# Adaptive modulation in a 256-token, ten-stage transformer kernel: from sums over partitions on TensorE to one fused multiply-and-add per 128 outputs on VectorE

## The chip, the cores and the metric

The kernel runs on one core of a Trainium2 chip, as one launch. The metric is the device time of that launch in microseconds. Each core has engines with queues of their own: TensorE (PE in the profile, its weight loads PEld), VectorE (DVE), ScalarE (ACT), GpSimd (POOL) and SyncE (SP, which only issues DMAs here). The engines wait for each other through counting semaphores.

## The reference

A sequence of 256 tokens with 1024 features passes through two layers of a first block (feed-forward, mixer, feed-forward) and two layers of a second block (mixer, feed-forward). The change is about the second block's modulation, which depends only on a vector `c` of 1024 numbers and not on the tokens:

```python
c_act = jax.nn.silu(c)
for l in range(DEPTH):                       # DEPTH = 2
    mod = (c_act @ w_ada[l] + b_ada[l])[:, None, :]      # w_ada[l]: 1024 x 6144
    shift_a, scale_a, gate_a, shift_f, scale_f, gate_f = jnp.split(mod, 6, axis=-1)
    h = rmsnorm(x, g_mix_pre[l]) * (1.0 + scale_a) + shift_a
    y = hybrid_mixer(h, ...)
    x = x + gate_a * rmsnorm(y, g_mix_post[l])
    h = rmsnorm(x, g_ffn_pre[l]) * (1.0 + scale_f) + shift_f
    x = x + gate_f * rmsnorm(swiglu_2(h, w_gate_up[l], w_down[l]), g_ffn_post[l])
```

The modulation's weight is 2 x 1024 x 6144 numbers of 4 bytes, 50 MB. Everything is float32.

## The kernel before

**Stages.** `STAGES` (line 21) lists ten: `f0 a0 f1 f2 a1 f3 b0 f4 b1 f5`. An `f` stage is a feed-forward (F = 2816, in 11 groups of 256), an `a` stage a mixer of the first block, a `b` stage one of the second. Tokens are two tiles of 128.

**Matmuls in three parts.** A float32 weight piece of 128 x 1024 (512 KB) is loaded by SP into one of six buffers `raw`. ScalarE copies it, rounded, to a high part (`Wh` or `QTh`, line 1253), VectorE subtracts to get the low part (`Wl` or `QTl`, line 1645), and TensorE multiplies three times (`three`, lines 820 to 822). SP may load the next piece into a buffer when VectorE has made its low part (`w_lo`). This splitting stream is most of the work of ScalarE and VectorE.

**Order.** It is written out by hand: `walk(s, engine)` gives the list of events of a stage for each engine. In an `f` stage the events are `gu` (gate and up product of a group and a token tile: 24 matmuls of 128x512 into PSUM bank 4 or 5), `turn` (two transposes by TensorE, line 886) and `down` (12 matmuls). There are 22 `gu` in a stage; `gu_in` numbers them 0 to 21. After a `gu` ScalarE takes the Silu (line 1332, function `gate`), VectorE multiplies by the up half (line 1738, `product`), TensorE turns the result, ScalarE (1356) and VectorE (1756) split it in two parts, and TensorE does `down`. The results of `turn` go to PSUM banks 6 and 7 in turn; `ring_no` numbers their uses, and the semaphore `f_z` says that a bank was read.

**Modulation.** It is spread over the four feed-forward stages k = 0 to 3 (`f0 f1 f2 f3`), half a layer in each. ScalarE's queue issues 24 loads of 512 KB in each of them (line 1318) into two buffers in `BT`. Such a load holds two blocks of 128 input rows by 512 outputs. VectorE multiplies a block by the Silu of c, one number for each partition, and adds it to `acc` (128 x 512; line 1727 for the first of eight blocks, line 1730 for the seven others). `ada_to(n)` says how many blocks are done by the n-th `gu`: 8 blocks for every 3 of them. After eight blocks `acc` still has to be summed over its 128 partitions: ScalarE makes a high part (1347), VectorE a low part (2070), TensorE multiplies both by a matrix of ones (`ada_sums`, lines 849 and 850, on one of the two `turn` banks), VectorE adds the bias (1749), and ScalarE's queue stores 512 numbers to a scratch row in HBM (1341). That makes 6 such groups in a stage, 24 in all. Before each `b` stage SP reads four rows of the scratch back as columns of 128 partitions x 8 (line 782), and VectorE's `columns` makes the scales out of them; the two gates are read back as rows (lines 796).

**Around it.** Before the weights of an `a` stage go on, SP waits for the modulation's last store (line 772 with the load at 775), as the buffers in `BT` are needed. At the start ScalarE loads `c` as 128 x 8 (line 1567) and takes its Silu (1569) before the first `turn_x`; the activation table is loaded there.

## Time and profile before

| | |
|---|---|
| Time, three runs | 1705.37, 1710.27, 1711.13 us; median 1710.27 us |
| Profiled execution, first to last instruction (span) | 1699.3 us |
| Own time of the profiled execution | not listed; the span is 11.0 us under the median of the three runs |
| Mean granted TensorE clock | 0.993 of full speed |
| Instructions | 22248 |
| HBM read | 327.32 MB, mean 193 GB/s |

A busy share is a mean over ten stages of different kinds. A matmul's row says when it started and how long it was in the engine; the next one starts before it ends, so the distance between two starts (here 0.22 to 0.23 us for 128x512) says what one more matmul costs, not its duration.

### The profile page before, as it was taken

The numbers are of one execution on the slowest core, as the hardware profiler recorded it, in microseconds if no ns is written. First come the engines' busy times: TensorE is split into PE (matmuls) and PEld (weight loads), VectorE is DVE, ScalarE is ACT, GpSimd is POOL, SyncE is SP. The second block draws the span as 40 slices with busy tenths as digits, with TensorE's granted clock in tenths as the row PEclk, the third lists the DMA queues.
The fourth block names the chain that finished last, engine by engine and source line by source line (L and its number), as shares of the span: only waits on it lengthen the run. The fifth ranks groups of instructions, "written<-read, shape, count | busy, mean of one in ns | idle before, by whom it ended". The sixth has DMA issues, their size and how long they took to land.

```text
span 1699.3 us, 22248 instructions
## 1 busy us (share of the span) xinstructions
PE 1633.9 (96%) x8104; PEld 1352.9 (80%) x8104; DVE 1194.3 (70%) x1833; ACT 930.5 (55%) x1789; POOL 90.6 (5%) x155
## 2 busy tenths in 40 slices
PE   8999998899999999999899999989999989999998
PEld 6888877688888888877688887778888878878887
DVE  6777688777776777779787776776655576675553
ACT  6445567654445444567664445766544367674342
POOL 0000111100000000021010000000000000010000
PEclk9999999999999999999999999989999999999999
DMA  8787633277866887734168784522665552246551
GB/s 321 266 294 260 222 104 124 87 266 256 275 233 207 276 275 257 244 111 144 51 231 273 260 273 144 180 100 87 211 198 175 169 180 94 100 155 222 198 181 62
DMA packets 100107, 329.87 MB, mean 194 GB/s; under 512 B 18800, under 2 KB 19312, under 8 KB 99488
## 3 DMA queue, kind: packets, MB, share of 16 engines
q1 hardware_dynamic: 85504, 276.59, 48.3%
q10 hardware_dynamic: 14496, 51.87, 9.2%
q8 instruction: 66, 1.08, 0.2%
q14 instruction: 41, 0.34, 0.1%
HBM read 327.32 MB, written 1.10 MB: 193 GB/s over the span
## 4 chain that ended last, share of the span: by engine, by line
PE 46%; DVE 6%; ACT 2%; POOL 1%; issue 1%; DVEq 0%; POOLq 0%; ACTq 0%
PE PS L820 14%; PE PS L822 14%; PE PS L821 13%; PE PS L974 1%; DVE Wl L1645 1%; PE PS L886 1%; DVE QTl L1645 1%; POOL st L2142 1%; PE PS L994 1%; DVE PTl L1841 1%; DVE st L1810 1%; PE PS L969 0%; PE PS L837 0%; ACT WK L1369 0%; ACT WK L1380 0%
## 5 line engine op out<-in xcount | busy, mean ns | idle before, releaser
L1645 DVE TENSOR_TENSOR Wl<-raw,Wh 128x1024 fp32r<-128x1024 f32 (+1 forms) x316 | 370.6, 1204 | 44.8 <-ACT Wh L1253 43.9
L820 PE MATMUL PS<-Wh,Hh 128*128 128x512 f32 (+2 forms) x936 | 368.4, 394 | 10.0 <-DVE Hl L1708 3.5
L822 PE MATMUL PS<-Wh,Hl 128*128 128x512 f32 (+2 forms) x936 | 363.3, 388 | 0.0
L821 PE MATMUL PS<-Wl,Hh 128*128 128x512 f32 (+2 forms) x936 | 362.9, 388 | 0.0
L1253 ACT ACTIVATE Wh<-raw 128x1024 fp32r<-128x1024 f32 (+1 forms) x316 | 316.9, 1041 | 24.1 <-DVE PTl L1756 11.0
L1645 DVE TENSOR_TENSOR QTl<-raw,QTh 128x1024 fp32r<-128x1024 f32 (+2 forms) x178 | 211.6, 1208 | 18.9 <-ACT QTh L1253 18.8
L820 PEld LDWEIGHTS PS<-Wh,Hh 128*128 128x128 f32 x936 | 176.8, 189 | 49.2 <-issue 7.5
L822 PEld LDWEIGHTS PS<-Wh,Hl 128*128 128x128 f32 x936 | 176.7, 189 | 36.0
L821 PEld LDWEIGHTS PS<-Wl,Hh 128*128 128x128 f32 x936 | 176.9, 189 | 33.7
L820 PE MATMUL PS<-QTh,Hh 128*128 128x512 f32 (+2 forms) x504 | 196.6, 390 | 3.8 <-DVE Hl L1708 3.8
L822 PE MATMUL PS<-QTh,Hl 128*128 128x512 f32 (+2 forms) x504 | 194.8, 387 | 0.0
L821 PE MATMUL PS<-QTl,Hh 128*128 128x512 f32 (+2 forms) x504 | 194.6, 386 | 0.0
L1332 ACT ACTIVATE WK<-PS,st 128x256 f32<-128x256 f32 x88 | 41.5, 472 | 264.1 <-PE PS L822 264.1
L1253 ACT ACTIVATE QTh<-raw 128x1024 fp32r<-128x1024 f32 (+2 forms) x178 | 181.4, 1043 | 7.4 <-DVE PTl L1756 5.5
L820 PE MATMUL PS<-Wh,PTh 128*128 128x512 f32 x320 | 132.3, 413 | 1.5 <-DVE PTl L1756 1.5
L1730 DVE SCALAR_TENSOR_TENSOR GQ<-BT,cact,GQ 128x512 f32<-128x512 f32 x168 | 125.8, 749 | 9.0 <-DMA BT<-in_ada 1.7
L1738 DVE SCALAR_TENSOR_TENSOR WK<-PS,st,WK 128x256 f32<-128x256 f32 x88 | 42.5, 482 | 120.7 <-ACT WK L1332 120.6
L822 PE MATMUL PS<-Wh,PTl 128*128 128x512 f32 x320 | 125.7, 393 | 0.0
L821 PE MATMUL PS<-Wl,PTh 128*128 128x512 f32 x320 | 124.9, 390 | 0.0
L820 PEld LDWEIGHTS PS<-QTh,Hh 128*128 128x128 f32 x504 | 94.7, 188 | 23.8 <-issue 3.1
L1334 ACT ACTIVATE WK<-PS 128x256 f32<-128x256 f32 x44 | 16.9, 384 | 175.9 <-PE PS L822 175.9
L822 PEld LDWEIGHTS PS<-QTh,Hl 128*128 128x128 f32 x504 | 94.6, 188 | 18.8
(232 smaller groups left out, 2529.3 us busy)
## 6 DMA issues: line engine op xcount, KB each, us to landing
raw<-in_ffn SPq DMA_DIRECT2D x396, 512.0 KB, 5.1
BT<-in_ada ACTq DMA_DIRECT2D x96, 512.0 KB, 4.3
raw<-in_win SPq DMA_DIRECT2D x64, 512.0 KB, 4.5
raw<-in_wo SPq DMA_DIRECT2D x32, 512.0 KB, 4.4
raw<-in_win SPq DMA_DIRECT2D x8, 420.0 KB, 3.8
BT<-in_nab SPq DMA_DIRECT2D x2, 1024.0 KB, 5.3
raw<-in_win SPq DMA_DIRECT2D x8, 256.0 KB, 2.7
BT<-in_t5b SPq DMA_DIRECT2D x2, 1024.0 KB, 4.9
```

The source lines that it names most:

```text
L820: e.matmul(out_, xh, wh, start=start, stop=False)
L821: e.matmul(out_, xh, wl, start=False, stop=False)
L822: return e.matmul(out_, xl, wh, start=False, stop=stop)
L886: ins = e.transpose(PS[:, 6 + z % 2, c * 128:c * 128 + 128], FA[:, n % 3, 1, c * 128:c * 128 + 128], ident)
L974: ins = e.matmul(at[k], ql if j == 2 else qh, kl if j == 1 else kh, start=j == 0 and it["group"] != "x", stop=j == 2)
L994: ins = e.transpose(PS[:, bank_of[key], col:col + 128], src[:, c * 128:c * 128 + 128], ident)
L1253: ins = e.activation(high(p)[:, 0:w], raw[p % RAW][:, 0:w], ACT.Copy)
L1332: ins = e.activation(FA[:, n % 3, 0, :], PS[:, 4 + n % 2, 0:256], ACT.Silu, scale=rms(s, t))
L1645: ins = e.tensor_tensor(low(p)[:, 0:w], raw[p % RAW][:, 0:w], high(p)[:, 0:w].bitcast(f32), ALU.subtract)
L1730: e.scalar_tensor_tensor(out=acc, in0=w, scalar=cact[:, c:c + 1], in1=acc, op0=ALU.mult, op1=ALU.add).then_inc(ada_step, 1)
L1738: ins = e.scalar_tensor_tensor(out=FA[:, n % 3, 1, :], in0=up, scalar=rms(s, t), in1=FA[:, n % 3, 0, :], op0=ALU.mult, op1=ALU.mult)
L1810: e.tensor_reduce(nm, src, AX.X, ALU.max, negate=True).then_inc(s_max, 1)
```

## The change

The weight is stored with its outputs on the partitions: piece u holds 128 outputs by all 1024 inputs, `ADA = 24` pieces in each of the four stages, 96 in all, each again one load of 512 KB. The Silu of c lies in every partition as a row of 1024 (`crow`). One `tensor_tensor_reduce` multiplies a piece by that row, sums along the row, starts the sum at the bias (new columns `ba` in the table `small`), and writes one column of `mods`. It writes its product over the piece. Sums by TensorE, the high and low part of `acc`, the bias addition, the 24 stores and 24 bias loads and the eight loads as columns fall away. What stays is a store of the gate of each half layer (128 x 8 numbers of 4 bytes, a number at a time) at the last `gate` of the stage, four in all. SP's waits at the `a` stage and in `columns` go by `ada_step`. At the start ScalarE no longer takes the Silu of a 128 x 8 tile; it loads `c` to all partitions after its first `gate` and takes the Silu of 128 x 1024 after its third. Numbers that the change leaves as they are: `ada_raw`'s two buffers and the pace of 8 half pieces, now 4 pieces, in 3 `gu`.

```diff
 def ada_to(n):
 
-    n = min(max(n - 2, 0), 18)
-    return 8 * (n // 3) + (0, 3, 6)[n % 3]
-
-
-def ada_done(n):
-
-    return range(ada_to(n) // 8, ada_to(n + 1) // 8) if n >= 0 else range(0)
+    return 4 * min(max(n - 2, 0), 18) // 3
...
-        oner = sb("oner", [128, 2], f32r)
         lfr = sb("lfr", [128, 2, 8], f32r)
         mhalf = sb("mhalf", [128, 32])
         st = sb("st", [128, 640])
-        cact = sb("cact", [128, 8])
-        mcol = sb("mcol", [128, 4, 8])
+        mods = sb("mods", [128, 2 * L * ADA])
+        mcol = sb("mcol", [128, 2, 8])
         ada_raw = BT[:, :, :, :].rearrange("p a b c -> p (a b c)").rearrange("p (s n) -> p s n", s=2)
-        acc = GQ[:, 0:ADA_N]
-        adab = GQ[0:1, ADA_N:2 * ADA_N]
-        acch = Vh[:, 0, 0:ADA_N]
-        accl = Vl[:, 0, 0:ADA_N]
+        crow = GQ[:, 0:D]
         OT = A[:, :, 0:D].rearrange("p t (c q) -> p t c q", q=128)
         PS = ctx.enter_context(nc.psum_tensor("PS", [128, 8, 512], f32))
         modd = nc.dram_tensor("mod_scratch", (L, 6 * D), f32, kind="Internal").ap()
...
                 if what == "a":
-                    e.wait_ge(mod_out, 16 * 6 * (2 * l + 1))
+                    e.wait_ge(ada_step, ADA * (2 * l + 1))
                     if l:
                         e.wait_ge(g_tab, l)
                     e.dma_start(GQ[:, 1728:1904], d["gq"][l]).then_inc(gq_in, 16)
                     e.dma_start(BT[:, :, :, :], d["nab"][l]).then_inc(bt_in, 16)
-                if what == "b":
-                    e.wait_ge(mod_out, 16 * ADA_G * (l + 1))
-                    if l:
-                        e.wait_ge(n_lo, 16 * (norm_no["f", 4] + 1))
-                    for i, k in enumerate((0, 1, 3, 4)):
-                        e.dma_start(mcol[:, i, :], modd[l, k * D:(k + 1) * D].rearrange("(c p) -> p c", p=128),
-                                    allow_slow_non_contiguous=True).then_inc(col_in, 16)
...
-            def ada_sums(g):
-
-                if g == 0:
-                    e.wait_ge(one_ok, 1)
-                e.wait_ge(ada_lo, g + 1)
-                z = ring_no["ada", g]
-                if z >= 2:
-                    e.wait_ge(f_z, z - 1)
-                ones = oner[:, 0:1].to_broadcast([128, 128])
-                e.matmul(PS[:, 6 + z % 2, 0:ADA_N], ones, acch, start=True, stop=False)
-                e.matmul(PS[:, 6 + z % 2, 0:ADA_N], ones, accl, start=False, stop=True).then_inc(ada_sum, 1)
 
...
-                        e.wait_ge(ada_step, 2 * u - 2)
+                        e.wait_ge(ada_step, u - 1)
                     e.dma_start(ada_raw[:, u % 2, :], d["ada"][u]).then_inc(ada_in[u % 2], 16)
                     state["ada"] += 1
 
             def gate(s, i, k, g, t):
                 n, f, p = gu_no[k, g, t], gu_in[k, g, t], ffn_at[k, "gu", g] + 3
                 if k < 4:
-                    ada_loads(min(24 * k + ada_to(f) // 2 + 2, 24 * k + 24))
+                    ada_loads(min(ADA * k + ada_to(f) + 2, ADA * (k + 1)))
                 if last_use[p] == (s, i):
                     e.wait_ge(w_used, freed[p] + 1)
                 else:
...
-            def modulation(k, f):
-
-                for x in ada_done(f - 2):
-                    x += 6 * k
-                    e.wait_ge(f_z, ring_no["ada", x] + 1)
-                    e.dma_start(modd[x // ADA_G:x // ADA_G + 1, x % ADA_G * ADA_N:(x % ADA_G + 1) * ADA_N], adab).then_inc(mod_out, 16)
-                for x in ada_done(f - 1):
-                    x += 6 * k
-                    e.wait_ge(ada_step, 8 * x + 8)
-                    if x:
-                        e.wait_ge(ada_sum, x)
-                    e.activation(acch, acc, ACT.Copy).then_inc(ada_hi, 1)
-                    if x:
-                        e.wait_ge(mod_out, 16 * x)
-                    e.dma_start(adab, d["b_ada"][x // ADA_G:x // ADA_G + 1, x % ADA_G * ADA_N:(x % ADA_G + 1) * ADA_N]
-                                ).then_inc(bias_in, 16)
+                if k < 4 and f == 21:
+                    e.wait_ge(ada_step, ADA * (k + 1))
+                    l, n = k // 2, 2 + 3 * (k % 2)
+                    e.dma_start(modd[l, n * D:(n + 1) * D].rearrange("(c p) -> p c", p=128), modulation(l, n),
+                                allow_slow_non_contiguous=True).then_inc(mod_out, 16)
 
...
-            e.dma_start(st[:, 0:8], d["c"]).then_inc(c_in, 16)
-            e.wait_ge(c_in, 16)
-            e.activation(cact[:, :], st[:, 0:8], ACT.Silu).then_inc(c_ok, 1)
-            e.wait_ge(one_set, 1)
-            e.activation(oner[:, :], st[:, 8:10], ACT.Copy).then_inc(one_ok, 1)
...
+                        if s == y == 0 and x == 0:
+                            e.dma_start(crow, d["c"].to_broadcast([128, D])).then_inc(c_in, 16)
+                        if s == y == 0 and x == 1:
+                            e.wait_ge(c_in, 16)
+                            e.activation(crow, crow, ACT.Silu).then_inc(c_ok, 1)
...
             def ada_steps(k, f):
-                for h in range(48 * k + ada_to(f), 48 * k + ada_to(f + 1)):
-                    u, c, g = h // 2, h % 8, h // 8
-                    w = ada_raw[:, u % 2, h % 2 * ADA_N:(h % 2 + 1) * ADA_N]
-                    if h % 2 == 0:
-                        e.wait_ge(ada_in[u % 2], 16 * (u // 2 + 1))
-                    if c == 0:
-                        if h == 0:
-                            e.wait_ge(c_ok, 1)
-                        if g:
-                            e.wait_ge(ada_lo, g)
-                        e.tensor_scalar(acc, w, cact[:, 0:1], None, ALU.mult).then_inc(ada_step, 1)
-                    else:
-                        e.wait_ge(ada_step, h)
-                        e.scalar_tensor_tensor(out=acc, in0=w, scalar=cact[:, c:c + 1], in1=acc, op0=ALU.mult,
-                                               op1=ALU.add).then_inc(ada_step, 1)
+                for u in range(ADA * k + ada_to(f), ADA * k + ada_to(f + 1)):
+                    w, l, j = ada_raw[:, u % 2, :], u // (2 * ADA), u % (2 * ADA)
+                    e.wait_ge(ada_in[u % 2], 16 * (u // 2 + 1))
+                    if u == 0:
+                        e.wait_ge(c_ok, 1)
+                    e.tensor_tensor_reduce(w, w, crow, 1.0, sm(f"ba{l}", j, j + 1), ALU.mult, ALU.add,
+                                           mods[:, u:u + 1]).then_inc(ada_step, 1)
 
...
-                if k < 4:
-                    for x in ada_done(f - 1):
-                        x += 6 * k
-                        e.wait_ge(ada_sum, x + 1)
-                        e.wait_ge(bias_in, 16 * (x + 1))
-                        z = ring_no["ada", x]
-                        e.tensor_tensor(adab, PS[0:1, 6 + z % 2, 0:ADA_N], adab, ALU.add).then_inc(f_z, 1)
...
-                e.wait_ge(col_in, 64 * (l + 1))
-                e.scalar_tensor_tensor(out=mcol[:, 1, :], in0=mcol[:, 1, :], scalar=1.0, in1=sm(f"pm{l}"), op0=ALU.add, op1=ALU.mult)
-                e.scalar_tensor_tensor(out=mcol[:, 3, :], in0=mcol[:, 3, :], scalar=1.0, in1=sm(f"pf{l}"), op0=ALU.add,
+                e.wait_ge(ada_step, 2 * ADA * (l + 1))
+                e.scalar_tensor_tensor(out=mcol[:, 0, :], in0=modulation(l, 1), scalar=1.0, in1=sm(f"pm{l}"), op0=ALU.add, op1=ALU.mult)
+                e.scalar_tensor_tensor(out=mcol[:, 1, :], in0=modulation(l, 4), scalar=1.0, in1=sm(f"pf{l}"), op0=ALU.add,
                                        op1=ALU.mult).then_inc(col_ok, 1)
...
-                        for g in ada_done(gu_in[k, x, y] - 1):
-                            e.wait_ge(ada_hi, 6 * k + g + 1)
-                            e.tensor_tensor(accl, acc, acch.bitcast(f32), ALU.subtract).then_inc(ada_lo, 1)
...
-    A["ada"] = np.concatenate([I["w_ada_2"][l].reshape(4, 2, 128, ADA_G, ADA_N).transpose(3, 0, 2, 1, 4)
-                               .reshape(ADA_G * 4, 128, 2 * ADA_N) for l in range(L)])
-    A["b_ada"] = I["b_ada_2"]
+    A["ada"] = np.concatenate([I["w_ada_2"][l].T.reshape(2 * ADA, 128, D) for l in range(L)])
     A["g_mix_post"] = I["g_mix_post_2"]
     A["g_ffn_post"] = I["g_ffn_post_2"]
     A["x"] = I["x"][0]
-    A["c"] = I["c_2"][0].reshape(8, 128).T
+    A["c"] = I["c_2"]
```

In the first `f` stage, TensorE's queue between the seventh `gu` and the `down` after it. Before:

```order
L820 MATMUL PS<-Wh,Hh 128x512
L821 MATMUL PS<-Wl,Hh 128x512
L822 MATMUL PS<-Wh,Hl 128x512
L849 MATMUL PS<-Vh,oner 128x512
L850 MATMUL PS<-Vl,oner 128x512
L886 MATMUL PS<-CT,WK 128x128 x2
L820 MATMUL PS<-Wh,PTh 128x512
```

Now, at the same place (lines 806 to 808 are `three`, line 857 is the `turn`):

```order
L806 MATMUL PS<-Wh,Hh 128x512
L807 MATMUL PS<-Wl,Hh 128x512
L808 MATMUL PS<-Wh,Hl 128x512
L857 MATMUL PS<-CT,WK 128x128 x2
L806 MATMUL PS<-Wh,PTh 128x512
```

The two sums over partitions are gone and nothing stands in their place; the same holds at the 23 other places.

VectorE's queue over one group of modulation in the same stage. Before:

```order
L1727 TENSOR_SCALAR GQ<-BT,cact 128x512
L1730 SCALAR_TENSOR_TENSOR GQ<-BT,cact,GQ 128x512 x2
L1738 SCALAR_TENSOR_TENSOR WK<-PS,st,WK 128x256
L1756 TENSOR_TENSOR PTl<-PS,PTh 128x256
L1730 SCALAR_TENSOR_TENSOR GQ<-BT,cact,GQ 128x512 x3
L1645 TENSOR_TENSOR Wl<-raw,Wh 128x1024 x2
L1645 TENSOR_TENSOR QTl<-raw,QTh 128x1024 x2
L1738 SCALAR_TENSOR_TENSOR WK<-PS,st,WK 128x256
L1756 TENSOR_TENSOR PTl<-PS,PTh 128x256
L1730 SCALAR_TENSOR_TENSOR GQ<-BT,cact,GQ 128x512 x2
L2070 TENSOR_TENSOR Vl<-GQ,Vh 128x512
```

Now (line 1680 is `tensor_tensor_reduce`, printed as `ISA`; line 1603 makes the low parts, 1688 is `product`, 1699 the low part of a `turn`):

```order
L1680 ISA BT,mods<-BT,GQ,SM 128x1024
L1680 ISA mods 128x1
L1688 SCALAR_TENSOR_TENSOR WK<-PS,st,WK 128x256
L1699 TENSOR_TENSOR PTl<-PS,PTh 128x256
L1680 ISA BT,mods<-BT,GQ,SM 128x1024
L1680 ISA mods 128x1
L1603 TENSOR_TENSOR Wl<-raw,Wh 128x1024 x2
L1603 TENSOR_TENSOR QTl<-raw,QTh 128x1024 x2
L1688 SCALAR_TENSOR_TENSOR WK<-PS,st,WK 128x256
L1699 TENSOR_TENSOR PTl<-PS,PTh 128x256
```

Each call is two instructions, one over 128x1024 and a second with 128x1 as its only operand. They stand where the blocks stood, ahead of the low parts of the same `gu`.

ScalarE's queue at the start of the program. Before:

```order
L1566 DMA X<-in_x 128x1024
L1567 DMA st<-in_c 128x8
L1569 ACT_TABLE_LOAD
L1569 ACTIVATE cact<-st 128x8
L1571 ACTIVATE oner<-st 128x2
L1285 ACTIVATE NW<-PS,SM 128x128
L1305 ACTIVATE Hh<-NW 128x128
```

Now, with the semaphores that each instruction waits for (`n_turn` comes from TensorE's first transposes):

```order
L1526 DMA X<-in_x 128x1024
L1256 ACT_TABLE_LOAD [waits n_turn]
L1256 ACTIVATE NW<-PS,SM 128x128 [waits sm0_in]
L1276 ACTIVATE Hh<-NW 128x128 [waits n_ya]
L1281 ACTIVATE Wh<-raw 128x512 [waits raw_in0]
```

The table load has moved behind the wait for the transposes. A second one now stands ahead of the first Silu of `gate` (line 1303), where there was none.

## Rows read from the trace of the kernel before

**Rows 1.** The page, busy time and share of the span.

```profile
PE 1633.9 (96%) x8104; PEld 1352.9 (80%) x8104; DVE 1194.3 (70%) x1833; ACT 930.5 (55%) x1789; POOL 90.6 (5%) x155
```

**Rows 2.** Windows in `f1`: length, then PE PEld DVE ACT POOL busy, PEclk, DMA, GB/s.

```profile
340.00:520.00 180.00, 180.00 (x817) 148.13 (x816) 136.38 (x183) 86.05 (x127) 0.75 (x2) 1.00 0.77 260
```

**Rows 3.** Timeline of PE around the first sum: start us, length us, what.

```profile
55.02 0.40 PE L849 MATMUL PS<-Vh,oner 128*128 128x512 f32 x1
...
55.25 0.39 PE L850 MATMUL PS<-Vl,oner 128*128 128x512 f32 x1
...
55.48 0.38 PE L886 MATMUL PS<-CT,WK 128*128 128x128 f32 x2
```

**Rows 4.** Timeline of PE, three `turn` in a row, the second behind a sum.

```profile
98.11 0.38 PE L886 MATMUL PS<-CT,WK 128*128 128x128 f32 x2
...
106.98 0.38 PE L886 MATMUL PS<-CT,WK 128*128 128x128 f32 x2
115.41 0.38 PE L886 MATMUL PS<-CT,WK 128*128 128x128 f32 x2
```

**Rows 5.** Groups on DVE by shape: count, busy us, mean ns, idle before.

```profile
L1645 DVE TENSOR_TENSOR Wl<-raw,Wh 128x1024 fp32r<-128x1024 f32 x303 | 360.0, 1220 | 43.0 <-ACT Wh L1253 42.3
...
L1730 DVE SCALAR_TENSOR_TENSOR GQ<-BT,cact,GQ 128x512 f32<-128x512 f32 x168 | 125.8, 749 | 9.0 <-DMA BT<-in_ada 1.7
...
L2070 DVE TENSOR_TENSOR Vl<-GQ,Vh 128x512 fp32r<-128x512 f32 x24 | 16.6, 693 | 16.8 <-ACT Vh L1347 16.8
L1749 DVE TENSOR_TENSOR GQ<-PS,GQ 1x512 f32<-1x512 f32 x24 | 16.0, 669 | 0.0
...
L1647 DVE SCALAR_TENSOR_TENSOR Wl<-raw,SM,Wh 128x1024 fp32r<-128x1024 f32 x12 | 15.0, 1280 | 1.9 <-ACT Wh L1255 1.9
...
L1727 DVE TENSOR_SCALAR GQ<-BT,cact 128x512 f32<-128x512 f32 x24 | 11.2, 468 | 0.0
...
L1898 DVE TENSOR_TENSOR st<-st 128x1 f32<-128x1 f32 x2 | 0.3, 159 | 0.1
```

**Rows 6.** Timelines of DVE and PE, late in `f0`: a `product` and its `turn`.

```profile
184.44 0.48 DVE L1738 SCALAR_TENSOR_TENSOR WK<-PS,st,WK 128x256 f32<-128x256 f32 x1
...
189.87 0.38 PE L886 MATMUL PS<-CT,WK 128*128 128x128 f32 x2
```

**Rows 7.** Timeline of ACT at the start.

```profile
1.65 1.28 ACT L1569 ACT_TABLE_LOAD   x1 [1.65 <-PEq L2403]
...
5.88 0.37 ACT L1285 ACTIVATE NW<-PS,SM 128x128 f32<-128x128 f32 x1 [0.64 <-PE PS L837]
```

**Rows 8.** Timelines of ACT, DVE and PE at the first `gate` and `product`.

```profile
21.97 0.45 ACT L1332 ACTIVATE WK<-PS,st 128x256 f32<-128x256 f32 x1
...
23.43 0.48 DVE L1738 SCALAR_TENSOR_TENSOR WK<-PS,st,WK 128x256 f32<-128x256 f32 x1
...
23.96 0.44 PE L886 MATMUL PS<-CT,WK 128*128 128x128 f32 x2 [2.00 <-DVE WK L1738]
```

**Rows 9.** Timeline of ACT, a table load in front of a Silu in `f4`.

```profile
1192.94 1.28 ACT L1334 ACT_TABLE_LOAD   x1
1194.23 0.38 ACT L1334 ACTIVATE WK<-PS 128x256 f32<-128x256 f32 x1
```

**Rows 10.** Issues and their SP row: small pieces between HBM and SBUF.

```profile
mcol<-mod_scratch SPq DMA_DIRECT2D x8, 4.0 KB, 4.1
...
L782 SPq DMA_DIRECT2D mcol<-mod_scratch x8: 379/712/2393, 1029.8 to 1356.0; - x8
```

**Rows 11.** Waits of SP's queue: us in total, times, longest us.

```profile
SPq L804 <- DVE Wl L1645: 907.3, 302, 21.9
...
SPq L775 <- DMA mod_scratch<-GQ: 9.6, 2, 4.8
```

**Rows 12.** Timelines at the end of `f0`: the low part, and the matmul after it.

```profile
198.44 0.42 DVE L1756 TENSOR_TENSOR PTl<-PS,PTh 128x256 fp32r<-128x256 f32 x1
...
199.39 0.48 PE L820 MATMUL PS<-Wh,PTh 128*128 128x512 f32 x1
```

More of the change, by code:

```diff
@@ L11 @@
 BIG = 1e30
-ADA_G, ADA_N = 12, 512
+ADA = 24
 PIECE = 1024
@@ L289, in columns_of, with modulation @@
                 return sm(f"f{k % 2 + 1}{k // 2}" if kind == "f" else f"mx{k}"), None
-            return (mcol[:, 3, :], mcol[:, 2, :]) if kind == "f" else (mcol[:, 1, :], mcol[:, 0, :])
+            if kind == "f":
+                return mcol[:, 1, :], modulation(k - 4, 3)
+            return mcol[:, 0, :], modulation(k, 0)
+        def modulation(l, n):
+            return mods[:, 2 * ADA * l + 8 * n:2 * ADA * l + 8 * n + 8]
         def scaled_x(s, t):
@@ L328, in program @@
         ada_in = [semaphore(f"ada_in{i}") for i in range(2)]
-        ada_step, ada_hi, ada_lo, ada_sum, bias_in, mod_out = (
-            semaphore(n) for n in ("ada_step", "ada_hi", "ada_lo", "ada_sum", "bias_in", "mod_out"))
-        tri_ok, one_set, one_ok, half_ok, c_ok = (semaphore(n) for n in ("tri_ok", "one_set", "one_ok", "half_ok", "c_ok"))
+        ada_step, mod_out = semaphore("ada_step"), semaphore("mod_out")
+        tri_ok, half_ok, c_ok = (semaphore(n) for n in ("tri_ok", "half_ok", "c_ok"))
         j_mm, j_act, j_dve = semaphore("j_mm"), semaphore("j_act"), semaphore("j_dve")
@@ L502, in program @@
                         gu_kept[k, x, y] = len(gu_kept)
-                    if k < 4:
-                        for g in ada_done(n - 1):
-                            ring_no["ada", 6 * k + g] = len(ring_no)
                     n += 1
@@ L764, in sp_program @@
                 hooks[first["a", l] + 8] = ("a", l)
-                hooks[first["b", l] + 4] = ("b", l)
                 hooks[first["b", l] + 12] = ("bt", l)
@@ L794, in sp_program @@
                         n = 5
+                    e.wait_ge(mod_out, 16 * (2 * l + (1 if what == "gate" else 2)))
                     post = d["g_mix_post" if what == "gate" else "g_ffn_post"]
@@ L875, in gate_up @@
                         ins.then_inc(f_mm, 1)
-                if k < 4:
-                    for x in ada_done(gu_in[k, g, t] - 1):
-                        ada_sums(6 * k + x)
             def turn(k, g, t):
@@ L1574, in act_program @@
                 for i, (what, x, y, z) in enumerate(ACT_WALK[s]):
-                    if what == "gu" and k < 4:
-                        modulation(k, gu_in[k, x, y])
                     weights(s, i)
```

14 lines of the change are left out of this document (7 added, 7 removed).

## The prediction

> **What bounds the kernel now.** I read the page of the profile first: TensorE is busy for 1633.9 of 1699.3 us, 96%, VectorE 70%, ScalarE 55% [rows 1]. A mean over ten stages says nothing of a single one, so I took the busy time by windows next: in a stretch of 180 us inside the feed-forward stage `f1`, TensorE is busy for all 180.00 us at full clock, VectorE for 136.38, ScalarE for 86.05, and the DMA engines for 0.77 of the time [rows 2]. The change touches the queues of the four stages `f0` to `f3`, and such stretches are most of them. There the length of TensorE's list is the time. Third I read TensorE's timeline at one of the sums, to see what an instruction costs there: the two matmuls of the sum start at 55.02 and 55.25 and the transposes after them at 55.48 [rows 3]. Each holds the queue for 0.23 us, though its own row says 0.40; the next one starts while it is still draining. None of them waited. Fourth, VectorE's groups by shape, for what goes and what could replace it [rows 5], and last the two ends of a stage and the start of the program, where TensorE does wait.
>
> **What the change removes from TensorE.** 24 pairs of matmuls. By the starts, a pair costs 55.48 - 55.02 = 0.46 us [rows 3]. A check that uses no duration: from one `turn` to the next it is 106.98 - 98.11 = 8.87 us with a sum between them and 115.41 - 106.98 = 8.43 without [rows 4], and the matmuls are otherwise the same, 24 of `gu` and 12 of `down`. The difference is 0.44. Between the two, 24 x 0.45 = 10.8 us. The durations would give 24 x 2 x 0.40 = 19 us, which is wrong for a pipelined engine and is not used. All 24 lie inside stretches like that of [rows 2], so I count the whole 10.8 us, -10.8.
>
> **What it changes on VectorE.** Gone: 125.8 + 11.2 us of multiply-and-add, 16.6 for the low part, 16.0 for the bias, 169.6 us in all, 42.4 in a stage [rows 5]. New: 96 calls. No row shows this instruction. The nearest is the one with two float32 tensors of 128x1024 and a number per partition, 1280 ns; without that number it is 1220 [rows 5]. So 1.22 us is the lower end for the main part if it takes one element at a time. The second instruction is small: 159 ns is what 128x1 takes [rows 5]. That gives 1.28 + 0.16 = 1.44 us for a call, 138 us in all, 31 less than before. The upper end: from 512 to 1024 elements the two shapes of multiply-and-add go from 749 to 1280 ns, 1.04 ns an element, so a program of two steps an element costs 1.28 + 1.06 + 0.16 = 2.5 us, and four steps 4.6. I take 1.44, the nearest row. Either way the value of VectorE's time here is nothing as long as it keeps up: the idle time in 180 us is 43.6 us [rows 2]. The point where it stops being free is 24 calls in 42.4 + 43.6 = 86 us, that is 3.6 us a call. Nor does the place hurt: before the densest `product` late in `f0` stood two multiply-and-adds and a low part; now two calls stand there, about the same length, and that product ended at 184.92 while its `turn` came at 189.87, a reserve of 5.0 us [rows 6]. 0.
>
> A page of the Trainium skill speaks against this instruction: "Vector Engine (DVE) Microarchitecture Reference", section "Points that are easy to get wrong", says that the scalar-tensor-tensor form with two sources in SBUF that are not bf16 runs at half throughput, since both read ports are taken and none is left to read back the accumulator. The rows of that form here, 749 ns for 512 elements and 1280 for 1024, are one element at a time, so for the form without an accumulator the trace disagrees; with one, no row exists. Its effect is the first rival below.
>
> **What it changes on ScalarE in the stages.** 24 copies of `acc` go, and with them their waits for VectorE; ScalarE is at 48% in [rows 2]. 0. What comes is a store of 1024 single numbers at the last `gate` of each stage. The same count of small pieces the other way took 379 ns to issue at the least, 712 in the middle, 2393 behind others, and 4.1 us to land [rows 10]. The shortest is that of the first in a batch, and here the queue has nothing in front of it, so I take 0.4 us. It falls where TensorE is tight: the last low part of `f0` ends at 198.86 and the matmul that needs it starts at 199.39, a reserve of 0.5 us [rows 12]. Part of the issue also lies beside the Silu in front of it. 0, with 4 x (2.4 - 0.5) = 8 us as the bad end.
>
> **What it changes on SP.** Its eight loads as columns go, and its two waits of 4.8 us for the modulation's last store at the `a` stages [rows 11]. SP waits for VectorE's low parts over 900 us in total [rows 11], so it is ahead of the weights' users. 0, and up to -2 us if an `a` stage starts sooner by it.
>
> **What it costs at the start.** Before, the activation table was loaded at 1.65, while everything waited for data, and ScalarE was then idle until the transposes came, 5.88 [rows 7]. In the new order the load waits for the same semaphore as the first work of ScalarE. It takes 1.28 us, and its follower starts 1.29 after its start [rows 9], so the chain through ScalarE, VectorE and the first matmul moves by +1.3 us. A second load stands in front of the first Silu of `gate`. That Silu would then end at 22.42 + 1.3 + 1.3 = 25.0; the `product` behind it started at 23.43, set by the low parts, which themselves move by 1.3 to 24.7; TensorE was already waiting there, 2.00 us [rows 8]. That is +0.3. The Silu over 128x1024 about 10 us later is 1 us of ScalarE in a place where it has reserve. Together +1.6. Bounds: +0.5 if a wait for a weight absorbs part of it, +2.6 if both loads count in full.
>
> On the same place the Trainium skill's page "ScalarE: Activation LUTs", section "What ACT_TABLE_LOAD costs", gives the same 1283 ns and adds about 1380 ns of drain for each change of table. By that figure the start would cost 2.8 us more; in this trace the follower starts 10 ns after the load [rows 9], so I leave it out.
>
> **The sum.** -10.8 + 1.6 = -9.2 us against the profiled execution: its span would go from 1699.3 to 1690.1. The median of the three runs is 11.0 us above that span; I assume that this stays. 1710.3 - 9.2 = 1701.1 us. That is 0.54% less.
>
> **The rivals.**
>
> *A call takes two steps an element.* 24 x 2.5 = 60 us in a stage in place of 42.4, so VectorE would be at 154 of 180 us: still under TensorE. But its slack of 5.0 us at a `product` shrinks where two calls and four low parts meet, and I give it 2 us of waits over the four stages: 1703. For it: the accumulator. Against it: the plain form's rows.
>
> *TensorE's time comes back as waits.* If `f` stages were paced by something just behind TensorE, the pairs would be worth nothing and the time would be 1710 + up to 1.6, say 1711. For it: DMA at 0.77 and VectorE at 0.76 of the window. Against it: 0.23 us from start to start without a gap, and 8.87 against 8.43. The case in which the change fails to do what it says is part of this: same time, with the sums gone.
>
> *The store of single numbers holds up the stage's end.* It is the one that would end slower. Place: the last `gate` of `f0` to `f3`, where the next stage's first weights and the last split compete. Price: each of four landings of 4.1 us [rows 10] turned into a stop, with the issue's wait, 16 us: -9.2 + 16 = +7, 1717. It decides from 2.3 us at each of the four ends. Against it: the weights are ahead [rows 11], and eight such loads stood in SP's own queue before.
>
> *VectorE becomes the bound.* From 3.6 us a call on each us costs 96 us; at 4.6 us it is +96 - 9 = 1797, at 3.8 +10. Against it: it takes four steps an element or a large fixed cost.
>
> **How the numbers follow.** Forecast 0.79; two steps an element 0.06; time given back 0.07; store 0.05; VectorE the bound 0.03. Around the forecast: start from +0.5 to +2.6, SP's waits up to -2, the pair by 0.44 or 0.46; three runs of one kernel lie 5.8 us apart, so a median may be off by 2 to 3. That makes 1696 to 1706 for the forecast alone; it holds the first rival too. The remaining 0.15 lies above, so with the forecast's own tails I put the range at 1695.5 to 1706.5. For this kernel about 0.3%, 5.1 us, is what can be told from no change. Faster: nearly all of the forecast and of the first rival, 0.82. Same: the time given back and the rest of those, 0.11. Slower: 0.07.
>
> **What would show it.** TensorE's two sum rows gone, and 8.43 us between all `turn` in the middle of a stage; each of `f0` to `f3` 2.7 us shorter, `f4` and `f5` unchanged; VectorE's busy time down by about 31 us; the call at 1.2 to 1.3 us and its second row at 0.1 to 0.2. The first Silu's table load at about 5.9 us and the first real matmul about 1.3 us later. The forecast is wrong if a call is over 2.5 us, if TensorE's idle time in `f1` and `f2` grows, or if the stage ends show TensorE waiting behind the store.

## The result, and the profile after

The changed kernel takes 1693.59 us (median of 5 runs, 1690.45 to 1694.38); the kernel before 1705.65 (5 runs, 1703.77 to 1711.13: the three already shown and two more). The ratio is 0.9927, 95% interval [0.9908, 0.9946]: faster, by 12 us or 0.7%. The forecast was 1701.1 us with a range from 1695.5 to 1706.5. The direction is right, the time lies 1.9 us below the range, and the kernel before had itself a median 4.6 us lower than the one shown.

The page after, its span and its busy times (answers to [rows 1]):

```profile
span 1692.6 us, 21864 instructions
...
PE 1626.7 (96%) x8056; PEld 1347.6 (80%) x8056; DVE 1146.9 (68%) x1784; ACT 914.8 (54%) x1765; POOL 90.8 (5%) x155
```

48 instructions less on TensorE, and 47 us less on VectorE where 31 were foretold. The 96 calls with their second rows come to 120.7 + 7.9 = 128.6 us in place of 169.6, so 41 of the 47 are theirs; the low parts of the weights take the same as before, 1219 and 1220 ns. The rest is overlap of neighbouring instructions, which the engine's total counts once: the rows of all groups together fall by 42 us. The groups on VectorE by shape:

```profile
L1680 DVE CUSTOM_DVE_ANT_0 BT<-BT,GQ,SM 128x1024 f32<-128x1024 f32 x96 | 120.7, 1276 | 0.0
...
L1680 DVE DVE_READ_ACCUMULATOR2_ANT mods<- 128x1 f32 x96 | 7.9, 82 | 0.0
```

The call takes 1276 ns; its second row (the accumulator's reading) takes 82, so 1.36 us together; the nearest rows gave 1280 and 159 [rows 5]. From start to start it holds the queue for 1.20 us. The window in `f1` that answers to [rows 2], with the same columns:

```profile
340.00:520.00 180.00, 180.00 (x818) 148.38 (x818) 125.72 (x175) 83.55 (x124) 1.37 (x4) 1.00 0.76 260
```

TensorE is still busy for all 180 us at full clock; VectorE fell from 136.38 to 125.72. Three `turn` in a row on PE (start, length), which answer to [rows 4]:

```profile
99.89 0.38 PE L857 MATMUL PS<-CT,WK 128*128 128x128 f32 x2
108.34 0.38 PE L857 MATMUL PS<-CT,WK 128*128 128x128 f32 x2
116.75 0.38 PE L857 MATMUL PS<-CT,WK 128*128 128x128 f32 x2
```

8.45 and 8.41: the step of 8.87 is gone. In this `f0` the plain steps take 8.45 and 8.41 in turn; from `f1` on, and in `f0` of the second profile below, they take 8.41, a little less than the 8.43 of before. The start, ACT and PE (answers to [rows 7, 8]):

```profile
5.77 1.28 ACT L1256 ACT_TABLE_LOAD   x1 [5.77 <-PE PS L823]
7.06 0.37 ACT L1256 ACTIVATE NW<-PS,SM 128x128 f32<-128x128 f32 x1
...
9.07 0.79 PE L806 MATMUL PS<-Wh,Hh 128*128 128x512 f32 x1 [2.53 <-DVE Wl L1671]
...
22.75 1.28 ACT L1303 ACT_TABLE_LOAD   x1
...
24.55 0.48 DVE L1688 SCALAR_TENSOR_TENSOR WK<-PS,st,WK 128x256 f32<-128x256 f32 x1 [0.38 <-ACT WK L1303]
...
25.09 0.44 PE L857 MATMUL PS<-CT,WK 128*128 128x128 f32 x2 [2.39 <-DVE WK L1688]
...
32.46 0.38 PE L857 MATMUL PS<-CT,WK 128*128 128x128 f32 x2
```

The first load stands behind the wait, as foretold. The first `turn` comes 1.1 us later than before, but the second 7.4 us after it, where it was 5.8 before. The windows of 26 to 30 and 285 to 315 us say why and hint at more:

```profile
26.00:30.00 4.00, 4.00 (x12) 3.09 (x12) 4.00 (x4) 4.00 (x7) 0.00 (x0) 0.58 0.94 311
...
285.00:315.00 30.00, 24.57 (x160) 21.27 (x161) 22.74 (x42) 22.05 (x59) 0.94 (x1) 0.83 0.11 36
```

PEclk (after the busy times) is 0.58 in the first and 0.83 in the second: part of each ran at the lower of TensorE's two levels, 1.2 GHz, after TensorE had waited. The kernel before has these:

```profile
26.00:30.00 4.00, 4.00 (x21) 3.29 (x20) 4.00 (x6) 2.85 (x5) 0.00 (x0) 1.00 0.95 329
...
285.00:315.00 30.00, 23.38 (x166) 20.12 (x167) 23.71 (x45) 23.25 (x64) 0.94 (x1) 0.94 0.11 36
```

So the two profiled spans, 1699.3 and 1692.6, differ by only 6.7 us, but the executions behind them differ in clock too. The store at a stage's end on ACT's queue, and the low part and the matmul that answer to [rows 12]:

```profile
195.81 0.42 ACTq L1310 DMA_DIRECT2D mod_scratch<-mods  x1
...
198.58 0.43 DVE L1699 TENSOR_TENSOR PTl<-PS,PTh 128x256 fp32r<-128x256 f32 x1
...
199.44 0.47 PE L806 MATMUL PS<-Wh,PTh 128*128 128x512 f32 x1
```

The issue is over 2.3 us before the low part, whose end at 199.0 leaves 0.4 us, as before.

### The profile page after: what moved, and what is told of

It reads as the page before. It is cut to its first block, busy times and chain, and to the rows that moved or that the text cites. A ratio compares the mean times of both kernels' runs of the same rounds, so it can differ in the third digit from the quotient of the medians.

```text
span 1692.6 us, 21864 instructions
## 1 busy us (share of the span) xinstructions
PE 1626.7 (96%) x8056; PEld 1347.6 (80%) x8056; DVE 1146.9 (68%) x1784; ACT 914.8 (54%) x1765; POOL 90.8 (5%) x155
## 4 chain that ended last, share of the span: by engine, by line
PE 45%; DVE 6%; ACT 3%; POOL 1%; issue 1%; DVEq 0%; POOLq 0%; ACTq 0%
PE PS L806 14%; PE PS L808 13%; PE PS L807 13%; PE PS L945 1%; DVE Wl L1603 1%; PE PS L857 1%; DVE QTl L1603 1%; POOL st L2081 1%; PE PS L965 1%; DVE PTl L1784 1%; DVE st L1753 1%; ACT WK L1329 1%; PE PS L940 0%; PE PS L823 0%; ACT WK L1340 0%
## 5 line engine op out<-in xcount | busy, mean ns | idle before, releaser
L1680 DVE CUSTOM_DVE_ANT_0 BT<-BT,GQ,SM 128x1024 f32<-128x1024 f32 x96 | 120.7, 1276 | 0.0
```

The lines of the kernel that those rows point to most:

```text
L1680: e.tensor_tensor_reduce(w, w, crow, 1.0, sm(f"ba{l}", j, j + 1), ALU.mult, ALU.add, mods[:, u:u + 1]).then_inc(ada_step, 1)
```

## The experiments

All medians are beside runs of the kernel before on the same chip: 1706.17 us for the first four kernels (23 runs), 1704.58 for the next four (22), 1703.51 for the last four (11).

**The kernel before, once more.**

> The kernel before once more, unchanged, for a second profile of it and its spread. Theory A (my forecast's base was off: the profiled execution of before, span 1699.3, was a quick one, and what differs between executions is the time that TensorE spends at its lower clock at the start and in the mixer stages): the span of each execution is its time less about 1.8 us as in the changed kernel's runs, not less 11.0, and this profile shows a span of 1702 to 1709 with lower clock in some mixer window that the first profile had at full clock. Theory B (a fixed 11 us lies around the span): span again near 1699 beside a time near 1710. Ratio 0.998 to 1.002 by both.

1704.9 us (12 runs), ratio 0.9982 [0.9964, 1.0], span 1700.9 of a time of 1702.71, a little under the 1702 to 1709 that theory A gave. Time less span is 1.8 us here and 1.8 to 2.1 in all other runs. So nothing stands for 11 us outside the span: the first profile was of one of this kernel's quicker executions, and two of the three shown times were among its longest (13 of the 56 runs beside the experiments reach 1710). What goes with the time is TensorE's mean granted clock: of the 56 runs of before beside the experiments those at 0.988 have spans of 1708 to 1711 us, those at 0.993 of 1698 to 1702. A line through the spans of all 146 runs of all kernels, with a constant for each kernel, falls by 12.6 us for 0.01 of clock and leaves 1.4 us. Its constants at 0.990 are what I call "at equal clock" below: before 1704.5, changed 1691.2, so -13.2. The standard error of such a constant is 0.2 us for the kernel before and 0.4 to 0.6 for the others with several runs. The measure is a rough one, because the same time at the lower level costs more in one place than in another: 10 us of it in `b0` go with 158.6 us from the last `turn` of `f3` to the first of `f4` in place of 154.5, and 10 us in `a0` with 160.7 us from `f0` to `f1` in place of 158.0.

**The sums cut to 16 columns.**

```diff
-e.matmul(PS[:, 6 + z % 2, 0:ADA_N], ones, acch, start=True, stop=False)
-e.matmul(PS[:, 6 + z % 2, 0:ADA_N], ones, accl, start=False, stop=True).then_inc(ada_sum, 1)
+e.matmul(PS[:, 6 + z % 2, 0:16], ones, acch[:, 0:16], start=True, stop=False)
+e.matmul(PS[:, 6 + z % 2, 0:16], ones, accl[:, 0:16], start=False, stop=True).then_inc(ada_sum, 1)
...
```

VectorE's bias addition reads the 16 columns over and over, so that its size stays; most of the modulation comes out wrong.

> The kernel before with the sums over partitions cut from 512 to 16 columns on TensorE (all but 16 of each 512 outputs of the modulation are then not summed over the partitions); VectorE, ScalarE and all DMAs as before. By my sum TensorE's part alone: the pair falls from 0.45 us to under 0.15, 24 times, -7 to -9 us, ratio 0.9947 to 0.996. Rival (the gain comes from VectorE's and ScalarE's relief, TensorE's time would have come back as waits): ratio 0.999 to 1.001.

1694.25 us (6 runs), 0.9914 [0.9896, 0.9931]; -9.6 at equal clock, more than either expectation. On PE:

```profile
55.52 0.17 PE L849 MATMUL PS<-Vh,oner 128*128 128x16 f32 x1
55.55 0.26 PE L850 MATMUL PS<-Vl,oner 128*128 128x16 f32 x1
55.66 0.44 PE L886 MATMUL PS<-CT,WK 128*128 128x128 f32 x2
```

A pair still holds the queue for 0.14 us in place of 0.46, and from first to last `turn` the stages `f0` to `f3` are 1.6 to 1.7 us shorter each, 6.6 in all. VectorE's and ScalarE's work is that of before, so columns on TensorE alone give at least half of the gain. The 3 us between 6.6 by stages and 9.6 at equal clock are open; that the low clock costs more in one stage than in another may hold a part of them, but that is not shown.

**The sums' columns put back into the changed kernel**, nothing else.

```diff
+if k < 4 and (gu_in[k, g, t] in (5, 8, 11, 14, 17, 20)):
+    h = high(ffn_at[k, "gu", g])
+    for c in range(4):
+        e.matmul(PS[:, 6 + z % 2, 256:512], Hh[:, 0, 0:128], Hh[:, c, :], start=c == 0, stop=c == 3)
```

> The changed kernel with TensorE's columns of the sums put back: at six turns of each of f0 to f3 four matmuls of 256 columns (1024 columns, as the two of 512), written to the half of the bank that no one reads, 24 places in all. VectorE, ScalarE and the DMAs stay as changed. Theory A (the gain is TensorE's): +10 to +11.5 us, 1704 to 1705, ratio to before 0.999 to 1.001; f1 to f3 longer by 2.7 us each, and 8.87 us in place of 8.43 between the turns with a sum. Rival B (3 us of the gain belong to the other engines): these stay, and the time comes out 1.5 to 3 us under before at an equal clock, ratio 0.998. Rival C (TensorE has slack and the sums were partly hidden): +3 to +6 us, 1697 to 1700.

1705.07 us (12 runs), 0.9994 [0.9979, 1.0009]: the gain is gone. Its PE:

```profile
109.68 0.38 PE L861 MATMUL PS<-CT,WK 128*128 128x128 f32 x2
118.09 0.64 PE L859 MATMUL PS<-Hh 128*128 128x256 f32 x4
118.56 0.38 PE L861 MATMUL PS<-CT,WK 128*128 128x128 f32 x2
```

8.88 us from `turn` to `turn`, and `f1` to `f3` 3.0 to 3.1 us longer each than changed. At equal clock it is 12.4 above the changed kernel (foretold 10 to 11.5) and 0.8 under before. Theory A stands, and rival C falls. Of rival B's 1.5 to 3 us 0.8 are left, with a standard error of 0.4; the stages bound it better, as `f1` to `f3` take 167.9, 167.9 and 167.5 us here and 168.0, 168.0 and 167.5 before.

**The changed kernel once more.**

> The changed kernel as it is, a second profile and more runs. Theory A (the change is worth 24 pairs of sums on TensorE, about -10.8 us, and +2.75 us at the start; what is left of the distance to the forecast comes from the base, and the spread of the runs from TensorE's granted clock in the mixer stages): ratio to before 0.993 to 0.996, and spans that lie 1.8 us under the times; at a mean clock of 0.990 a span of 1691 us. The stages f1 to f3 again 187 to 188.3 us, f4 and f5 again 196.6 and 199.2. Rival B (a part of the gain, about 3 us, comes from VectorE's and ScalarE's shorter lists): cannot be told from A by this run alone; it gives the base for the three others.

1692.59 us (6 runs), 0.9919 [0.9897, 0.994], span 1690.6. In this execution the clock did not fall after the first `turn`:

```profile
25.28 0.44 PE L857 MATMUL PS<-CT,WK 128*128 128x128 f32 x2 [2.13 <-DVE WK L1688]
31.06 0.38 PE L857 MATMUL PS<-CT,WK 128*128 128x128 f32 x2
```

5.8 us between them, as before, and both 1.3 us later than in the first profile of before. The kernels with an early table load vary too: leaving out the last two kernels below, their first `turn` comes at 23.96 to 25.08 us (six profiles, mean 24.4), that of the six with late loads at 25.09 to 25.57 (mean 25.3). So the late loads cost some 0.9 us on average, and the stretch at the lower clock 1.6 more where it appears. It appears behind late loads in three profiles of six and behind an early one in two of six (the first step from `turn` to `turn` is then 7.3 to 7.4 us in place of 5.8), so these profiles do not tie it to the loads. In the five TensorE had waited 1.99 to 2.47 us before the first `turn`, in the others 0 to 2.14.

**The late table loads alone, in the kernel before** (both small activations moved behind the first `gate`s, so that the first load stands behind a wait).

```diff
-e.wait_ge(c_in, 16)
-e.activation(cact[:, :], st[:, 0:8], ACT.Silu).then_inc(c_ok, 1)
...
+if s == y == 0 and x == 1:
+    e.wait_ge(c_in, 16)
+    e.activation(cact[:, :], st[:, 0:8], ACT.Silu).then_inc(c_ok, 1)
```

> The kernel before with the changed kernel's start alone: the Silu of c (128 x 8) moved behind ScalarE's third gate, so that the activation table is loaded behind the wait for the first transposes and again before the first gate. By my sum +1.6 us. By theory A +2.8 us, since TensorE waits 0.4 us longer for the first product and its clock then falls to the lower level for the next matmuls, as the changed kernel's trace shows at 26 to 29 us. Rival: absorbed, 0.

1706.52 us (12 runs), 0.9996 [0.9978, 1.0014]. The `turn`s come at 25.3, 31.1 and 39.5 us, 1.4 later than in the first profile of before and 1.1 than in the second; the clock does not fall there. At equal clock it is +0.3. The price is there in the trace and below what the time can tell.

**The early table load, in the changed kernel.**

```diff
+e.wait_ge(one_set, 1)
+e.activation(st[:, 12:14], st[:, 8:10], ACT.Silu)
...
+e.memset(st[:, 8:10], 1.0).then_inc(one_set, 1)
```

> The changed kernel with a Silu of two constants put at the very start of ScalarE's list, so that the table is loaded while everything waits for data and no load stands at the first transposes or the first gate. Theory A: the changed kernel less 2.8 us at the start (first turn of group 0, token tile 1 at 29.7 us in place of 32.5), which is 1690 to 1691 where the changed kernel takes 1693.6, and lower-clock stretches in the mixer stages that may come or go though no instruction there was touched. By my sum: less 1.6. Ratio to before 0.990 to 0.992.

1689.68 us (6 runs), 0.9884 [0.9864, 0.9904]: the lowest median of all. The load is back at the start:

```profile
1.17 1.28 ACT L1528 ACT_TABLE_LOAD   x1 [1.17 <-PEq L2344]
...
8.51 0.79 PE L806 MATMUL PS<-Wh,Hh 128*128 128x512 f32 x1 [1.82 <-DVE Wl L1673]
```

The first matmul comes 0.56 us earlier than in the changed kernel's first profile and the first `turn` at 24.4. The second comes 7.4 us after it: here too the clock falls, though the load is early. At equal clock the kernel is at -0.7 against the changed one, with a standard error of 0.7; it beats before, but that it beats the changed kernel is not shown.

**VectorE's work nearly doubled.**

```diff
+own.mark(e.tensor_tensor(w, w, crow, ALU.mult))
+own.after()
 e.tensor_tensor_reduce(w, w, crow, 1.0, sm(f"ba{l}", j, j + 1), ALU.mult, ALU.add, mods[:, u:u + 1])
```

> The changed kernel with a second instruction of 128x1024 on VectorE in front of each of the 96 calls (the weight's tile multiplied by the row once more, so the modulation comes out with c squared; the output is another). It adds 96 x 1.2 = 117 us of VectorE, so that a step takes 2.6 us in place of 1.36, under the 3.6 us from which VectorE was said to decide. Theory A (VectorE's time is free up to there): within 0.1% of the changed kernel, 1693.6 us; f1 to f3 longer by under 0.3 us each. Rival B (VectorE's relief of 47 us gave some 3 us of the gain): it gives at least these 3 us back, more by proportion (117 / 47 x 3 = 7 us): 1697 to 1701, seen as longer f1, f2, f3 and as waits of TensorE for products.

1700.87 us (11 runs), 0.9964 [0.9947, 0.998]; +6.9 at equal clock over the changed kernel. Here the rival was right. The window in `f1`, then one of the places where it is lost, DVE and PE around the third `turn` of `f1`:

```profile
340.00:520.00 180.00, 179.51 (x811) 147.00 (x810) 153.35 (x195) 83.07 (x123) 1.15 (x4) 1.00 0.77 260
```

```profile
364.01 1.22 DVE L1603 TENSOR_TENSOR Wl<-raw,Wh 128x1024 fp32r<-128x1024 f32 x1
...
365.15 0.48 DVE L1690 SCALAR_TENSOR_TENSOR WK<-PS,st,WK 128x256 f32<-128x256 f32 x1
...
365.37 0.38 PE L857 MATMUL PS<-CT,WK 128*128 128x128 f32 x2
365.54 0.42 DVE L1701 TENSOR_TENSOR PTl<-PS,PTh 128x256 fp32r<-128x256 f32 x1
...
366.01 0.50 PE L806 MATMUL PS<-Wh,PTh 128*128 128x512 f32 x1 [0.26 <-DVE PTl L1701]
```

VectorE is busy for 153 of 180 us, far from full, and yet TensorE waits: VectorE works its queue in order, each pair in it holds 2.5 us in place of 1.2, and so the low part `PTl` was ready, at 365.96, only when the matmul that reads it had been held up by some 0.5 us (the step around it takes 8.94 us in place of 8.41). The same low part in the changed kernel, second profile:

```profile
363.50 0.41 DVE L1699 TENSOR_TENSOR PTl<-PS,PTh 128x256 fp32r<-128x256 f32 x1
...
364.73 0.48 PE L806 MATMUL PS<-Wh,PTh 128*128 128x512 f32 x1
```

Ready at 363.91, needed at 364.73: 0.8 us in reserve. There are four such places in each of `f1` to `f3` (0.53, 0.33, 0.34 and 0.53 us), 1.7 a stage, and 1.3 in `f0`: 6.6 in all, nearly the 6.9. And the kernel before had passed this point already. The same two rows there:

```profile
365.30 0.42 DVE L1756 TENSOR_TENSOR PTl<-PS,PTh 128x256 fp32r<-128x256 f32 x1
...
365.77 0.50 PE L820 MATMUL PS<-Wh,PTh 128*128 128x512 f32 x1
```

Ready at 365.72 and read at 365.77, without a reserve. This step of `f1` to `f3` takes 8.52 to 8.57 us in the kernel before, still 8.49 to 8.53 where only TensorE's columns were cut, and 8.41 in the changed kernel, also with the sums' columns put back. That is 0.1 to 0.16 us a stage won by VectorE's relief.

**Without the four stores of the gate** (SyncE reads its rows from x).

```diff
-if k < 4 and f == 21:
-    e.wait_ge(ada_step, ADA * (k + 1))
-    ...
-    e.dma_start(modd[...], modulation(l, n), ...).then_inc(mod_out, 16)
```

> The changed kernel without the four stores of the gate at the ends of f0 to f3; SyncE reads its gate rows from x, which is there from the beginning (the gate's values are other ones, so the output is too). Theory A (the store costs nothing, a reserve of 0.5 us stands against an issue of 0.4): within 0.05%, 1693 to 1694. Rival (the store holds up each stage's end by 0.5 to 2 us, and the forecast's sum was right in the middle of the stages only): -2 to -8 us, 1686 to 1691.5, with f0 to f3 each 0.5 to 2 us shorter.

1690.44 us (6 runs), 0.991 [0.9888, 0.9932]. That median is 2.1 us under the changed kernel's beside it, the edge of what the rival gave, but these runs had the higher clock: at equal clock -0.1 (standard error 0.7). The stages decide: from first to last `turn` `f1` to `f3` take 164.9, 164.9 and 164.4 us with and without the stores, and from the last `turn` of `f1` to the first of `f2` 22.1 us without and 22.1 and 22.3 in the two profiles with them. The stores cost nothing that shows.

**Why the plain step is 0.02 us shorter, in `f4` and `f5` too.** Two looks at the kernel before: with its tensors at the changed kernel's places in SBUF, and with its semaphores numbered as there.

```diff
+              (f"ba{_l}", 48)]
...
-oner = sb("oner", [128, 2], f32r)
...
+mcol = sb("mcol", [128, 4, 8])
 cact = sb("cact", [128, 8])
-mcol = sb("mcol", [128, 4, 8])
+oner = sb("oner", [128, 2], f32r)
...
```

```diff
-col_in = semaphore("col_in")
...
 d_own, a_own, p_own = semaphore("d_own"), semaphore("a_own"), semaphore("p_own")
+col_in = semaphore("col_in")
+ada_hi, ada_lo, ada_sum, bias_in = (semaphore(n) for n in ("ada_hi", "ada_lo", "ada_sum", "bias_in"))
+one_set, one_ok = semaphore("one_set"), semaphore("one_ok")
```

> The kernel before, with its tensors at the places in SBUF that they have in the changed kernel: the table of small vectors is 96 numbers longer, and the removed small tensors stand at the end. The instructions are those of before. Asked: why each step of a feed-forward stage takes 8.43 us before and 8.41 in the changed kernel, in f4 and f5 too, where nothing was edited. If the place of the tensors does it, the steps of f4 and f5 take 8.41 here. If not, 8.43.

> The kernel before, with its seven removed semaphores (ada_hi, ada_lo, ada_sum, bias_in, col_in, one_set, one_ok) allocated last, so that all others have the numbers that they have in the changed kernel. The instructions are those of before. If the numbers of the semaphores give the 0.02 us of a step, those of f4 and f5 take 8.41 here. If the programs of the engines themselves do, 8.43.

Two `turn`s in `f5`, first with the new places, then with the new semaphores:

```profile
1615.04 0.38 PE L887 MATMUL PS<-CT,WK 128*128 128x128 f32 x2
1623.45 0.38 PE L887 MATMUL PS<-CT,WK 128*128 128x128 f32 x2
```

```profile
1616.35 0.38 PE L887 MATMUL PS<-CT,WK 128*128 128x128 f32 x2
1624.78 0.38 PE L887 MATMUL PS<-CT,WK 128*128 128x128 f32 x2
```

8.41 and 8.43: in `f4` and `f5` the places do it, the semaphores don't. In `f0` to `f3` of the first, most plain steps take 8.45, and `f1` takes 168.3 us in place of 168.0, so there the places alone do not explain the changed kernel's 8.41; which tensor it is stays open. One run each, 1707.12 and 1700.21 us, says nothing of their times.

**TensorE kept at work in its waits**, from the version with the early table load: first only before the first `turn`, then in the two `a` stages too.

```diff
+if z == 0:
+    for x in range(14):
+        e.matmul(PS[:, 6, 256:512], Hh[:, 0, 0:128], Hh[:, x % 8, :], start=x == 0, stop=x == 13)
```

```diff
+if p in (2, 3, 5):
+    e.wait_ge(tri_ok, 1)
+    spare = {2: 4, 3: 10, 5: 8}[p]
+    for x in range(spare):
+        e.matmul(PS[:, b, 0:S], IM[:, 0, :], IM[:, :, :].rearrange("p a b -> p (a b)"), ...)
```

> The changed kernel with the table load at the start again (an early Silu of two constants), and 14 matmuls of 256 columns that no one reads in front of the first turn, where TensorE waited 2.0 us. Theory: it is this wait, after the others of the first 25 us, that is followed by the stretch at the lower clock from 25.4 to 28.8; with it filled the second turn comes 5.8 us after the first, not 7.3, in every execution: -1.4 us against the same kernel without them, 1688.3. Rival: the stretch depends on the 8 us before, or comes later all the same: no change, or +0.2 if the matmuls take longer than the wait.

> As the last one, and also matmuls that no one reads in the two a stages, in the bank that the next values are to be written to: 4, 10 and 8 of 256 columns before the value products 2, 3 and 5, where TensorE waited 0.8, 1.4 and 1.2 us from start to start. Theory (the spread of the runs is TensorE's clock, which falls after waits): the stretches at the lower clock behind them (6.8 to 10.2 us in a0, 6.8 in a1) get fewer, -1 to -5 us, and the times lie closer together. Rival: the longest wait of these stages, 2.4 us before the third turn of queries and keys, is not filled, so the stretches stay: 0 to +0.5 us.

The first, on PE:

```profile
22.71 1.83 PE L857 MATMUL PS<-Hh 128*128 128x256 f32 x14
24.63 0.44 PE L860 MATMUL PS<-CT,WK 128*128 128x128 f32 x2
30.40 0.38 PE L860 MATMUL PS<-CT,WK 128*128 128x128 f32 x2
```

The second `turn` comes 5.8 us after the first, where it was 7.4 without them: the stretch is gone in this profile. But the median is 1691.89 us (6 runs), 0.9928 [0.9912, 0.9943], no better than without, and not the 1688.3 of the theory; at equal clock -0.2. The second gives 1691.55 (6 runs), 0.992 [0.9902, 0.9939]: in its profile less of `a0` and `a1` ran at the lower level than in the first's, but more of `b0`. There the window of the second kernel, then that of the changed one's second profile:

```profile
1110.00:1145.00 35.00, 31.10 (x180) 28.60 (x179) 19.54 (x33) 17.52 (x55) 1.61 (x5) 0.71 0.34 121
```

```profile
1110.00:1145.00 35.00, 30.21 (x206) 27.46 (x204) 21.48 (x38) 20.16 (x67) 2.24 (x6) 0.85 0.34 121
```

The theory that filling a few waits makes the time better isn't borne out; what puts a stretch in one stage or another is open.

## Why the prediction was wrong in its time

**The step that failed is the base**: "The median of the three runs is 11.0 us above that span; I assume that this stays." It doesn't. Of the miss of 7.5 us, 4.6 are this: 1710.27 us was the median of three runs, and that of the five, with two more, 1705.65; the three sets of the 56 later ones have 1703.5 to 1706.2. The time of an execution is its span and 1.8 us. The shown times hinted at it: 1705.37 to 1711.13 beside a profile of 1699.3 is a spread of over 10 us. From a base of 1705.65 the same sum gives 1696.4, and the range moved down by 4.6 us (1690.9 to 1701.9) holds the 1693.59. The sum was -9.2 and the measured difference 12.1 us, at equal clock 13.2: the other 2.9 us are terms that were too small or set at 0, below. By the traces the `f` stages lost 13.0 us and the start cost 0.9 to 1.3, which makes 11.7 to 12.1.

**TensorE's term, -10.8: right.** Pairs at 0.45 us by starts, all 24 on the path; the sums put back returned 12.4 us, their columns alone cut gave 6.6 to 9.6. By first to last `turn`, `f0` to `f3` lost 3.0, 3.1, 3.1 and 3.1 us (foretold: 2.7), and `f4` and `f5` 0.3 and 0.4 (foretold: 0). In `f1` that is 6 x 0.45 = 2.7 from the sums, 0.16 from the step in which VectorE's low part was late, and 12 x 0.02 = 0.24 from the shorter plain steps. Over six stages the two last come to 13.0 - 10.8 = 2.2 us, which no term had. For `f4` and `f5` the runs show the tensors' places as the cause of the shorter step; for `f0` to `f3` its cause is open.

**VectorE, 0: near, for a wrong reason.** The call takes 1276 ns, with 82 for the accumulator, as long as the plain form that goes one element at a time (1.28 us, [rows 5]), and the first rival (two steps an element) fell with it. The Trainium skill states half throughput for the scalar-tensor-tensor form in "Vector Engine (DVE) Microarchitecture Reference", section "Points that are easy to get wrong"; the trace disagrees, if this call, printed as `CUSTOM_DVE_ANT_0`, is of that form, which the trace does not tell. Its effect was set at 0 and was -0.3 to -0.4 us, three steps of 8.52 to 8.57 us that now take 8.41. Wrong is the point of 3.6 us a call "where it stops being free": that was an average over the stage, and at 2.5 us TensorE already paid 7 us. The reserve of 5.0 us at one `product` [rows 6] was not the smallest; the smallest, at the third `turn` of a stage, I had not looked at. The first rival, priced at 2 us of waits, would have cost about 7.

**The store, 0: right.** The issue took 0.42 us and leaving the store out changed no stage. The rival fell: it needed 2.3 us at each of four ends.

**SP, 0 to -2: 0.** Its waits of 4.8 us at the `a` stages are gone. These stages' lengths follow the clock, but profiles can be paired in which it falls at nearly the same places: from the last `turn` of `f0` to the first of `f1` it is 160.7 us in the changed kernel (first profile) and in before with late loads, and from `f2` to `f3` 164.6 in the latter and in the changed kernel with the columns put back. Nothing was won there.

**The start, +1.6: right in its mechanism, and too high.** The load stands behind the wait, and late loads put the first `turn` at 25.3 us on average where early ones put it at 24.4: 0.9 us, and 1.3 against the profile that the prediction read. The `turn` after it came 2.7 us later where the clock fell. The follower of the first load starts 10 ns after it (7.06 after 5.77 + 1.28), and the second load, at 22.75, 0.02 us after the end of the copy before it. By this the 1380 ns of drain in the Trainium skill's "ScalarE: Activation LUTs", section "What ACT_TABLE_LOAD costs", did not show here either. What I had left out is that TensorE's wait before the first `turn` can be followed by a stretch at the lower level, 7.4 in place of 5.8 us; but it followed with early loads too, so it is no price of the change that the runs show.

**The time given back as waits:** fell; nothing came back, and the columns alone, put back, cost 12.4 us.

## What to carry over

A gain on a saturated TensorE is well read from start to start of its matmuls, and from the same step with and without the piece; a forecast of the time must start from the spread of many executions and the clock of the profiled one, not from one median and one span. Whether VectorE's time is free is read at the tightest meeting point of its queue with TensorE's, not from its idle share: at 85% busy it cost 7 us. Watch the first use of each activation function: where its table load stands behind a wait, an idle early slot for it is cheap to give, though its gain here, under 1 us, is within the spread of the runs.

## What the runs showed of the hardware

- TensorE's mean granted clock differs between executions of one kernel (0.987 to 0.996 for the kernel before), and so do their spans, by 13.5 us (1697.3 to 1710.8), 0.8%. In the profiles these are stretches at 1.2 GHz: in the four mixer stages, where TensorE had just waited 0.9 to 2.4 us, at the very end, and in five profiles behind the first `turn`. They lie at other places from one execution to the next.
- The store of 1024 single numbers from 128 partitions to HBM landed after 11.5 us (10.9 to 12.1); the loads of the same pieces the other way had taken 4.1 [rows 10].
- The place of tensors in SBUF moved the step of a stage by 0.02 us of 8.43, with the same instructions: down in `f4` and `f5`, up for most steps of `f1` to `f3`.
- A pair of matmuls of 16 columns took 0.14 us from start to start, a third of a pair of 512 (0.46).
